# Hymba-style decoder step on one core: two convolution chunks in each of the first two attention steps, output projection begun inside the last one, parameter and expert-weight loads moved and spread

## What is computed

```python
proj = x @ w_in + b_in                     # q, k, v (768 columns), ca, cg (1024)
attn = sliding-window attention with rotary q, k and a sink per head
u    = ca * sigmoid(cg)
conv = silu(layer_norm(depthwise_causal_conv(u, 31 taps)))
mix  = concat([attn, conv]) @ w_out + b_out
h    = layer_norm(alpha * x + mix)
# router: best of 4 groups, then 2 of its 8 experts (32 in all)
y    = layer_norm(alpha * h + sum over 2 experts of gate * (silu(h @ w1) * (h @ w3)) @ w2)
```

## Time and profile before

| what | value |
|---|---|
| runs | 1673.23, 1678.99, 1673.23 us; median 1673.23 |
| the profiled execution | 1676.19 us, its span 1674.4 us |
| mean granted TensorE clock | 0.93 of full |
| PE busy | 1442.2 us, 86% of the span |
| DVE, ACT, POOL busy | 547.8, 376.8, 404.2 us |
| stage 1 | 9.5 to 248.5 us |
| stage 2 | to 639.8 us |
| stage 3 | 655.1 to about 998 us |
| stages 4 and 5 | about 1011 us to the end |

### The profile page before, as it was taken

One profiled execution on the slowest core, in us unless ns is written; L12 is line 12 of the kernel. 1 busy time (PEld: TensorE's weight loads), 2 busy tenths in 40 slices (PEclk: granted clock), 3 DMA queues, 4 the chain that ended last, 5 costly groups with the idle time before them and its releaser, 6 DMA issues.

```text
span 1674.4 us, 19234 instructions
## 1 busy us (share of the span) xinstructions
PE 1442.2 (86%) x5253; PEld 763.3 (46%) x5254; DVE 547.8 (33%) x1815; ACT 376.8 (23%) x730; POOL 404.2 (24%) x594
## 2 busy tenths in 40 slices
PE   7999992989999985787999957999999999999800
PEld 3444430656666651344555544445455454544300
DVE  0111110554555552346666540111111111111174
ACT  0000000234444442023334311121121121111112
POOL 3000000000000002335555431233333332323258
PEclk9999995999999996988999968999999999999955
DMA  8333322121222154653233223997768777888573
GB/s 351 94 93 95 97 77 62 59 68 64 66 81 69 57 176 118 234 197 145 104 127 126 95 76 115 370 351 189 231 175 284 221 206 244 246 285 263 119 274 139
DMA packets 86158, 269.80 MB, mean 161 GB/s; under 512 B 16288, under 2 KB 34984, under 8 KB 72966
## 3 DMA queue, kind: packets, MB, share of 16 engines
q1 hardware_dynamic: 63422, 216.22, 36.0%
q0 software_dynamic: 14912, 50.37, 12.9%
q10 hardware_dynamic: 7760, 2.43, 0.6%
HBM read 205.72 MB, written 66.45 MB: 163 GB/s over the span
## 4 chain that ended last, share of the span: by engine, by line
PE 45%; issue 41%; DMA 5%; DVE 3%; POOL 3%; POOLq 1%; DVEq 1%; ACT 0%; SPq 0%; ACTq 0%
PE P L812 11%; PE bank_S L830 9%; PE bank_S L734 7%; PE P L734 6%; PE M L812 5%; PE bank_T L800 3%; DMA work<-h_rows,idx 2%; PE M L752 2%; POOL big L1516 2%; DMA big<-in_w 1%; DVE big L1383 1%; DMA work<-conv_rows 1%; PE bank_T L743 1%; POOLq L1395 1%; PE M L820 1%
## 5 line engine op out<-in xcount | busy, mean ns | idle before, releaser
L812 PE MATMUL P<-big,work 128*128 x512 | 227.0, 596 | 2.4 <-ACT work L1001 2.4
L569 PE MATMUL P<-big,work 128*128 128x256 f32 (+3 forms) x544 | 184.3, 496 | 0.0
L830 PE MATMUL bank_S<-big,work 128*128 x384 | 177.4, 606 | 1.8 <-DVE work L1344 1.8
L1413 POOL TENSOR_SCALAR lnx<-lnx 128x1024 f32<-128x1024 f32 x1 | 2.8, 2821 | 633.5 <-DMA lnx<-in_b_out 633.5
L812 PEld LDWEIGHTS P<-big,work 128*128 128x128 f32 x512 | 97.8, 191 | 125.6 <-issue 125.6
L569 PEld LDWEIGHTS P<-big,work 128*128 128x128 f32 (+1 forms) x544 | 99.6, 186 | 79.1 <-issue 71.0
L1404 POOL TENSOR_TENSOR tick<-tick 1x1 f32<-1x1 f32 x249 | 42.6, 193 | 328.7 <-DMA tab<-slot_rows 158.6
L1344 DVE COPY work<-M 128x256 f32<-128x256 f32 x48 | 20.4, 424 | 295.9 <-PE M L820 295.9
L734 PE MATMUL bank_S<-big,work 128*128 128x512 f32 x256 | 115.1, 603 | 0.0
L734 PE MATMUL P<-big,work 128*128 128x512 f32 x256 | 113.3, 595 | 0.0
L812 PE MATMUL M<-big,work 128*128 x256 | 112.5, 592 | 0.0
(11 more groups left out here) (227 smaller groups left out, 1915.2 us busy)
## 6 DMA issues: line engine op xcount, KB each, us to landing
big<-in_w SPq DMA_DIRECT2D x96, 1024.0 KB, 5.0
work<-in_xt_prompt SPq DMA_DIRECT2D x32, 512.0 KB, 3.4
big<-in_toe SPq DMA_DIRECT2D x16, 512.0 KB, 3.4
work<-in_x_prompt SPq DMA_DIRECT2D x16, 512.0 KB, 4.1
h_rows<-work SPq DMA_DIRECT2D x16, 512.0 KB
sum_rows<-work SPq DMA_DIRECT2D x16, 512.0 KB
big<-sum_rows SPq DMA_DIRECT2D x16, 512.0 KB, 8.2
out_y_prompt<-big SPq DMA_DIRECT2D x16, 512.0 KB
```

The lines of the kernel that those rows point to most:

```text
L569: last = mm(dst[0:n, 0:c1 - c0], lhs[:, k, :], w_qkv[:, k, c0:c1], start=(k == 0), stop=(k == KD - 1))
L812: last = mm(UP[j][:, :].rearrange("p (m f) -> p m f", m=2), xgT[:, k, :], both[:, k], start=(k == 0), stop=(k == KD - 1))
L830: last = mm(bank_S[:, half * 512:(half + 1) * 512], gT[:, k, :], wmem[:, bass.ds(off + 2 * KD * FF + k * D + half * 512, 512)], start=(k = ...
```

## The change

- The keys and the state are loaded by POOL, right after its first memsets. `Ks` lies in the columns of ptB; the first two `toe` chunks are issued at conv_in tile 3.
- The input bias is two loads, into other columns (`b_conv`, `b_qkv`). `ln_g` and `ln_b` are loaded in step 3, `b_out` in step 17.
- Chunks 0 and 1 run in step 0, 2 and 3 in step 1, then one chunk a step up to chunk 15 in step 13. In step 0 the projections come first. The store of the convolution and the load of `w_out` move from step 16 to step 13.
- The sample tile's convolution chain is done in steps 7 to 11, that of c = 1 in steps 16 and 17. `project_out(0)` and `turn_z(1)` stand in step 17, `project_out(1, 0)` before the last `values`. c = 1 uses the banks of c = 0.
- The expert matrices are issued one by one: the first three in steps 15 to 17, the other nine at c = 1 to 9, each behind the x load of its c.

```diff
+        OUT = [PAIR[0]] + [PAIR[c % 2 == 0] for c in range(1, NT + 1)]
+        CHUNK_OF = [(0, 1), (2, 3)] + [(step + 2,) for step in range(2, CHUNKS - 2)]
+        CHUNK_OF += [()] * (STEPS - len(CHUNK_OF))
...
             for i, tile in enumerate(CONV_IN):
                 load_xT(i + 2)
+                if i == 3:
+                    load_toe(0)
+                    load_toe(1)
...
-            sp.dma_start(Ks[0:WIN - 1], a["cache_k"][:, 1:WIN, :].rearrange("b s n -> s b n")).then_inc(s["s_cache"], 16)
...
-            load_toe(0)
-            load_toe(1)
...
             for step in range(STEPS):
                 t = step - 2
+                if step == NT + 2:
+                    sp.wait_ge(s["last_out"], 48)
+                    after(sp, s["pe_T"], NT - 1)
+                    load_x(1)
                 if 0 <= t - 1:
                     after(sp, s["at_ev"], t - 1)
                     sp.dma_start(at_dram[t - 1], at_sb).then_inc(s["at_st"], 16)
...
-                if step + 2 < CHUNKS:
-                    load_toe(step + 2)
-                if step == NT + 2:
+                for chunk in CHUNK_OF[step]:
+                    if chunk + 2 < CHUNKS:
+                        load_toe(chunk + 2)
+                if step == 3:
+                    sp.dma_start(ln_g, a["ln1_g"].partition_broadcast(P)).then_inc(s["ln1_in"], 16)
...
-                if step == CHUNKS:
+                if CHUNKS - 1 in CHUNK_OF[step]:
                     sp.wait_ge(s["cv_ev"], CHUNKS)
...
+                if step == NT - 1:
+                    load_conv(1)
+                    load_conv(2)
+                if NT - 1 <= step <= NT + 1:
+                    load_matrix(0, 0, step - (NT - 1))
                 if step == NT + 1:
...
+                    sp.dma_start(bx, a["b_out"].partition_broadcast(P)).then_inc(s["ln1_in"], 16)
+                    load_x(0)
+                    after(sp, s["pe_x"], 2 * NT + 1)
+                    load_attn(1)
+                    load_attn(2)
...
-                if c == 1:
-                    load(0, 0)
-                    load(1, 1)
-                if c == 3:
-                    sp.wait_ge(s["cvd_st1"], 64)
-                    load(2, 2)
-                    load(3, 3)
+                if 1 <= c <= 3 * (WR - 1):
+                    if c == 4:
+                        sp.wait_ge(s["cvd_st1"], 64)
+                    load_matrix(1 + (c - 1) // 3, 1 + (c - 1) // 3, (c - 1) % 3)
...
+                if step == NT + 1:
+                    after(pe, s["q_ev"], NT)
+                    after(pe, s["kv_ev"], NT)
+                    pe.wait_ge(s["w_out_in"], 16)
+                    project_out(0, 0, "pe_o0")
+                    project_out(0, 1, "pe_o1")
...
+            project_out(1, 0, "pe_o0")
+            after(pe, s["ptB_ev"], NT - 1)
+            values(NT - 1, 1, ptB).then_inc(s["pe_vB"], 1)
+            for c in range(1, NT + 3):
...
+            g.dma_start(Ks[0:WIN - 1], a["cache_k"][:, 1:WIN, :].rearrange("b s n -> s b n")).then_inc(s["s_cache"], 16)
```

More of the change, by code:

```diff
@@ L233, in layer @@
         flat_ptB = ptB.rearrange("p i w t -> p (i w t)")
-        zlin, zsig = (view(flat_ptB[:, CH * i:CH * (i + 1)], c=CC, t=P) for i in range(2))
+        zl = sb("zl", 2 * CH)
+        zlin, zsig = (view(zl[:, CH * i:CH * (i + 1)], c=CC, t=P) for i in range(2))
         mixT = [view(b, k=KD, t=P) for b in xT]
@@ new lines, in load, with load_conv @@
+            def load(e, q):
+                for m in range(3):
+                    load_matrix(e, q, m)
+            def load_conv(c):
+                tile = OUT_IN[c]
+                if tile == NT:
+                    return
+                after(sp, s["z_ev"], c - 2)
+                sp.wait_ge(s["cvd_st0"], 64)
+                if tile >= 4:
+                    sp.wait_ge(s["cvd_st1"], 64)
+                sp.dma_start(cn[c % 2], conv_dram[P * tile:P * (tile + 1), :]).then_inc(s[f"cn_in{c % 2}"], 16)
@@ new lines, in load_attn, with load_x @@
+            def load_attn(c):
+                tile = OUT_IN[c]
+                if tile == NT:
+                    return
+                if c > 2:
+                    after(sp, s["pe_o1"], c - 2)
+                sp.wait_ge(s["at_st"], 16 * (tile + 1))
+                sp.dma_start(mixT[c % 2][:, 0:G, :].rearrange("p g t -> p (g t)"), at_dram[tile]).then_inc(s[f"am_in{c % 2}"], 16)
+            def load_x(c):
+                tile = OUT_IN[c]
+                after(sp, s["o1_ev"], c - 2)
+                src = a["x_sample"] if tile == NT else a["x_prompt"][P * tile:P * (tile + 1), :]
+                sp.dma_start(xb[c % 2][0:rows_of(tile), :], src).then_inc(s[f"xr_in{c % 2}"], 16)
@@ L718, in turn_z @@
-            def turn_z(c):
+                elif step == 9:
+                    turn_z(0, M0)
+            SAMPLE_DONE = {9: ("zl_ok", 1), 2: ("sA_ev", 2), 3: ("s_exp", 1), 4: ("sD_ev", 1), 5: ("s_fin", 1), 6: ("sN_ev", 1)}
+            def turn_z(c, bank=M1):
                 n = rows_of(OUT_IN[c])
@@ L728, in project_out @@
                 lhs = mix_of(c)
+                after(pe, s[f"o{half}_ev"], 0 if c == 1 else c - 2)
                 for k in range(KD):
@@ L760, in rank @@
                 mm(M0[:, 64 + NE:64 + 2 * NE], C["ones"][0:n, :], ohs[0:n, :], start=True, stop=True).then_inc(s["pe_rk"], 1)
-            after(pe, s["at_ev"], NT - 1)
-            after(pe, s["cv_ev"], CHUNKS - 1)
-            after(pe, s["q_ev"], NT)
-            after(pe, s["kv_ev"], NT)
-            turn_z(0)
-            pe.wait_ge(s["w_out_in"], 16)
-            for c in range(NT + 3):
-                if c <= NT:
-                    after(pe, s["o0_ev"], c - 2)
+            pe.wait_ge(s["const_in"], 16)
@@ L1395, in _ @@
             g.drain()
+            g.dma_start(Ks[0:WIN - 1], a["cache_k"][:, 1:WIN, :].rearrange("b s n -> s b n")).then_inc(s["s_cache"], 16)
+            for i in range(2):
+                src = a["state_conv"].rearrange("(i b) j n -> i (b j) n", i=2)[i]
+                g.dma_start(state_n[0:NROW, i], src).then_inc(s["s_state"], 16)
             col = [1]
```

392 lines of the change are left out of this document (192 added, 200 removed).

## The result

The change makes the kernel faster. Four runs of the changed kernel have a median of 1603.97 us (1601.57 to 1608.36), four of the kernel before beside them 1673.23 us (1665.66 to 1678.99): a ratio of 0.9592, with a 95% interval of 0.9547 to 0.9636. The profiled execution took 1601.57 us with a span of 1599.7 us; 1602.0 and 1600.2 were forecast.

What follows compares the result with a forecast made beforehand. PE bounds the kernel, busy 86% of the span, so its waits and low-clock stretches count. 28 + 0.2 - 3 - 0.5 + 24.5 + 27 - 2 = 74.2 us saved, giving 1599.0 us; range 1586 to 1628.

Steps and rivals of the forecast that it cites:

- Start of the steps: Last conv_in matmul to first transpose of step 2: 67.7 us before, 39.8 with the change, saving 28.
- The first wait stays: Rival: PE in step 0 still waits for something until 280 us, so the 28 us stay: 1627 us; chance 0.04.
- Two chunks fewer in steps 14 and 15: Steps 14 and 15: chunks there cover waits, so of 2.5 us per step only 0.2 in all returns, at most 2.6.
- Store of the convolution in step 13: Store holds SP, delaying step 14's attention store and holding ACT about 8 us in step 15: cost 3 us, ends 0 and 8.
- Sample tile's chain: Steps 7 to 11: four small PE transposes and one wait for DVE cost 0.5 us.
- Passage: Last scores to `project_out(2)`: 63.0 us becomes 38.5, waits of 5.33 and 15.34 gone; saves 24.5, ends 29 and 19.
- Expert matrices one by one: `project_out(2)` to `project_out(6)`: 29.0 us available, 2 lost over nine c; saves 27, ends 29 and 13.
- the waits move to DVE's chain: Rival: late convolution rows and worst-case matrices lose 16 us at nine c, 5.5 in the passage: 1620.5 us; chance 0.17.
- Start-up: Keys and state, 988 KB, run from about 16 us beside loads PE waits for: cost 2 us, ends 0 and 5.
- The early key load holds an engine: Rival, start-up: POOL's key load occupies one engine, delaying every start-up transfer; PE stands some 18 us: 1617 us; chance 0.08.
- The clock: Rival: PE's clock falls to 1.2 GHz after long unbroken work, costing 114 us among the experts: 1713 us; chance 0.02.
- The three signs of being wrong: PE waits 10+ us in first 60 us; DVE's conv-row waits reach PE at c = 2-10; experts' stage changes length.

## Why the prediction was right

The three large terms were right in place, size and cause: 28.3, 24.9 and 24.1 us where 28, 24.5 and 27 were forecast. Moving the loads back brought the first wait, bundling the matrices the second; the third, the passage, was tested only in part.

- *Start of the steps.* 39.4 us against 39.8, wait by wait: 1.57, 0.78 and 2.14 us where 1.5, 0.8 and 2.5 stood. "The first wait stays" fell.
- *Two chunks fewer in steps 14 and 15.* Step 14 takes 19.50 us against 19.57, in line with the 0.2 us; in step 15 the hold covers it. The run with one chunk in each step adds what the sum left out: the doubled chunks also have the rows ready for step 16, which is worth 15 us of wait.
- *Store of the convolution in step 13.* Right in the chain (SP, attention store, ACT, PE), and near the 8 us end: 6.1 against 3. Mis-sized were two things: ACT was held for 10.35 us, not 8, and the lower clock behind the wait, some 2 us in step 16, was in no term.
- *Sample tile's chain.* Step 9 takes 20.1 us, 0.5 above its neighbours, as forecast. Steps 2 and 4 took 2.0 us more than before for no term of mine, at a lower clock: step 2 behind the wait for the matrix of chunk 4, whose 2.5 us I had counted without it, step 4 behind a wait of 3.7 us that both kernels have (granted clock 0.87 there, 0.93 before).
- *Passage.* 24.9 against 24.5, and the two waits behind it 2.04 and 1.40 against 2 and 1.6. But the reason that I gave for the 5.33 us, that `project_out(0)` fills the softmax, is worth 1 to 3 us by the run without it.
- *Expert matrices one by one.* 24.1 against 27. The nine c cost nothing one by one: I had given a matrix up to 5.0 us ahead of the rows, its time to landing, but SP hands it over in 0.43 us. What I had missed is the single load of the rows of c = 3 in the passage, 11.24 us late for DVE. It costs 4 to 6 us by the run that moved it. This is in small what the rival "the waits move to DVE's chain" described, at one c instead of nine.
- *Start-up.* The term that was mis-sized most: 6.3 us against 2, beyond its end of 5. I had costed the key load by its bytes, 988 KB at the pace of a large transfer. It ran beside the activation tile's load, landed only at 74 us, and took turns with the tile on one engine; and, not seen at all, the bias was cut in two, whose packets stood ahead of the constants on ACT's queue.
- *The early key load holds an engine.* Right in cause, refuted in size. The keys' 4 KB packets run one behind another, as on one engine, and the tile's last eight packets took turns with them. But they only took turns: holding the load back gained 5.3 us, not the 18 by which that case differs. I gave this case 0.08; the forecast held beside it only because its price was small, and that is luck. The rule that I weighed against it (the Trainium skill, DMA: Bandwidth & Descriptors, "Why a DMA increments its semaphore by 16 and not by 1") gives sixteen engines to some direct copies that POOL issues, and not to all, as I had put it. This trace does not bear it out for the data of this load, which took 41.9 us to landing even where it was held to a quieter time.
- *The clock.* No slice fell without a wait ahead of it; the case of 1713 us fell.

The three signs of being wrong in my last sentence all came, taken at their word. PE does wait for 17.2 us in the first 60, though 11.6 of them stood in the kernel before as well; it should have said more than 10 us of new waits. One wait of DVE for convolution rows did turn into a wait of PE, 2.72 us at c = 3, and that was a true miss. And the experts' stage was 11.1 us shorter in the first two profiles, of which the spread between executions makes the larger part. The upper end of the range, by its own terms, is 1629 and not 1628.

Down to the first gather, the terms missed by -4.3, +0.3, -2.1, -3.1, +0.4, -2.9 and +1.2 in the order of the table, 10.5 us less saved than forecast; the experts' 11.1 us filled the gap. Without them the trace gives 63.6 us, and that is what the series with more runs measured: 1668.51 - 1605.13 = 63.4 us. So the gain is nearer to 64 us than to 74, and the first comparison's 1673.23 us for the kernel before lay high.

## What to carry to other kernels

A queue that is held for 20 us costs nothing by itself; ask which small transfer stands behind it and who needs that one. Spreading large loads one per period, and moving a slow one to a queue where nobody stands behind it, won 24 and 22 us (of the 22, the start-up took 6 back), and 4 to 6 us more came from asking for rows as soon as their buffer is free rather than in loop order. Cost a transfer by the pace at which its like was measured and by how many engines carry it, not by its bytes, and add to a wait the slow clock that follows it.

## What the runs showed of the hardware that I had not expected

The same key load of 127 rows goes out from POOL as 127 packets of 4 KB, one behind another at 0.20 us each, with 1905 packets of 32 bytes beside them, and from SP as packets of 0.5 KB, 405 of them in 10 us at 21 GB/s. Either way its data moves at the pace of one engine. While it ran, a 512 KB activation load took 20.8 us from issue to use (25.55 to 46.37), against 14.9 and 15.0 without it, though the engines were not full in the second half of that time: their mean share was 0.71 from 32 to 36 us, 0.55 to 40 and 0.29 to 46. One busy engine of 16 delays a transfer that is spread over all of them, and the mean share does not show it.

What a short wait costs in clock varies. Step 2 follows a wait of 2.1 to 2.5 us in every variant of the changed kernel, yet it took 22.1 us in two profiles of it and 23.9 to 24.4 in seven variants, at the lower level of the clock for a longer part of it (from the wait's end to the end of the step, the mean granted clock was 0.93 in the changed kernel and 0.87 with the key load held).
